# The last stage of a two-layer trunk (combine of two expert rows, final norm): rolled with two buffers, or written out with sixteen

## What is computed

```python
# end of hier_moe, layer 1: each token's two expert rows, weighted, are added to the residual x
x = x + hier_moe(h, ...)
# and then the final norm
inv = lax.rsqrt(jnp.mean(x * x, axis=-1, keepdims=True) + 1e-6)
y = x * inv * final_norm
```

## Time and profile before

| | us |
|---|---|
| median of 3 runs | 3452.34 |
| the 3 runs | 3441.14, 3452.34, 3454.4 |
| span of the profiled execution | 3440.8 |

### The profile page before, as it was taken

One profiled execution on the slowest core, in us unless ns is written; L12 is line 12 of the kernel. 1 busy time (PEld: TensorE's weight loads), 2 busy tenths in 40 slices (PEclk: granted clock), 3 DMA queues, 4 the chain that ended last, 5 costly groups with the idle time before them and its releaser, 6 DMA issues. The chain is left out here.

```text
span 3440.8 us, 53421 instructions
## 1 busy us (share of the span) xinstructions
PE 2953.7 (86%) x16322; PEld 2534.4 (74%) x16323; DVE 1949.2 (57%) x2787; ACT 1384.3 (40%) x2388; POOL 950.1 (28%) x894
## 2 busy tenths in 40 slices
PE   6999999999999999769999589999959589999700
PEld 5887788778877887658888489888849478889600
DVE  6548754876387638732211555576647777665433
ACT  5334333433343334321111145666624256666411
POOL 1013200320032003300000144465624256554332
PEclk8999999999999999979999689999979789999955
DMA  5323332323232323253222467798667569987555
GB/s 185 107 86 109 97 112 80 110 97 112 79 108 99 117 74 110 99 172 102 106 98 86 141 217 277 281 323 317 245 210 261 181 237 323 330 301 280 180 184 196
DMA packets 332189, 587.33 MB, mean 171 GB/s; under 512 B 23104, under 2 KB 206912, under 8 KB 332096
## 3 DMA queue, kind: packets, MB, share of 16 engines
q1 hardware_dynamic: 294944, 450.92, 38.3%
q0 software_dynamic: 37152, 135.28, 11.0%
HBM read 427.27 MB, written 158.86 MB: 170 GB/s over the span
## 5 line engine op out<-in xcount | busy, mean ns | idle before, releaser
L57 PE MATMUL ret_ps_p<-ret_w_hi,ret_x_hi 128*128 128x512 f32 x1536 | 606.7, 395 | 15.6 <-DVE ret_x_lo L1077 12.6
L59 PE MATMUL ret_ps_p<-ret_w_hi,ret_x_lo 128*128 128x512 f32 x1536 | 600.0, 391 | 0.0
L58 PE MATMUL ret_ps_p<-ret_w_lo,ret_x_hi 128*128 128x512 f32 x1536 | 599.2, 390 | 0.0
L1077 DVE TENSOR_TENSOR ret_x_lo<-hT,ret_x_hi 128x1024 fp32r<-128x1024 f32 x193 | 368.4, 1909 | 249.9 <-ACT ret_x_hi L1017 248.4
L57 PE MATMUL moe_ps_gu<-moe_gu_hi,moe_x_hi 128*128 128x256 f32 x1520 | 431.7, 284 | 3.5 <-DVE moe_x_lo L553 2.8
L58 PE MATMUL moe_ps_gu<-moe_gu_lo,moe_x_hi 128*128 128x256 f32 x1520 | 429.1, 282 | 0.0
L59 PE MATMUL moe_ps_gu<-moe_gu_hi,moe_x_lo 128*128 128x256 f32 x1520 | 429.1, 282 | 0.0
L985 POOL TENSOR_TENSOR ret_state_lo<-ret_state,ret_state_hi 128x1024 fp32r<-128x1024 f32 x68 | 176.6, 2597 | 838.2 <-ACT ret_state_hi L1007 838.2
L463 POOL TENSOR_TENSOR moe_dn_lo<-moe_raw_down,moe_dn_hi 128x1024 fp32r<-128x1024 f32 x128 | 366.5, 2881 | 17.7 <-ACT moe_dn_hi L498 16.9
L57 PEld LDWEIGHTS ret_ps_p<-ret_w_hi,ret_x_hi 128*128 128x128 f32 x1536 | 289.4, 188 | 77.2 <-DVE ret_x_lo L1077 14.4
L59 PEld LDWEIGHTS ret_ps_p<-ret_w_hi,ret_x_lo 128*128 128x128 f32 x1536 | 289.1, 188 | 61.7
(11 more groups left out here) (220 smaller groups left out, 5630.6 us busy)
## 6 DMA issues: line engine op xcount, KB each, us to landing
moe_raw_gate<-in_moe_w_gate SPq DMA_DIRECT2D x64, 1024.0 KB, 7.4
moe_raw_up<-in_moe_w_up SPq DMA_DIRECT2D x64, 1024.0 KB, 10.9
moe_raw_down<-in_moe_w_down SPq DMA_DIRECT2D x64, 1024.0 KB, 10.3
expert_rows<-moe_y POOLq DMA_DIRECT2D x95, 512.0 KB, 7.5
raw<-in_ret_w_in SPq DMA_DIRECT2D x20, 1024.0 KB, 9.0
qk_rows<-ret_qk_out SPq DMA_DIRECT2D x64, 256.0 KB, 2.1
ret_qk_out<-qk_rows SPq DMA_DIRECT2D x64, 256.0 KB, 3.0
gate_rows<-ret_gate SPq DMA_DIRECT2D x64, 256.0 KB, 2.0
```

Source lines behind the costliest of these rows:

```text
L57: pe.matmul(out, x_hi, w_hi, start=first, stop=False)
L58: pe.matmul(out, x_hi, w_lo, start=False, stop=False)
L59: return pe.matmul(out, x_lo, w_hi, start=False, stop=last)
L1077: dve.tensor_tensor(x_lo[par][:, :, :], hT[:, :, ds(t * P, P)], x_hi[par][:, :, :].bitcast(F32), ALU.subtract).then_inc(x_split, 1)
```

## The change

`final_phase` no longer uses `Combine`. It has buffers of its own for each of the 16 tiles: `x_res`, `picked0`, `picked1` (64 KB of each partition each), and 16 columns each of `sumsq`, `mean_eps` and `rstd`. All 16 tiles are written out on every engine. Gathers read their row numbers from `row_of_token` itself, so `index` and its copies are gone. Loads and gathers of tiles 0 to 3 are issued at the start, those of tile t+4 as soon as the second multiply-add of tile t is done. The multiply-adds and the norm write into `x_res`, the squares go to `picked0`, and the store reads `x_res`; no buffer is used twice.

```diff
-        comb = Combine(s, x_in_rows, y_rows, weight, row_of_token, gain)
+        x_res = s.slots("x_res", TILES, [P, D])
+        picked = [s.slots(f"picked{k}", TILES, [P, D]) for k in range(TOPK)]
...
         @blk.sync
         def _(sp):
-            comb.load_gain(sp)
-            comb.load(sp, 0, 0)
-
-            def step(i, par, has):
-                if has[0] and not (isinstance(i, int) and i >= TILES - 1):
-                    comb.load(sp, i + 1, 1 - par)
-                if has[1]:
-                    sp.wait_ge(y_ready, i)
-                    sp.dma_start(out[ds((i - 1) * P, P), :], y[1 - par][:, :]).then_inc(y_stored[1 - par], 16)
-            staggered(sp, step, 2)
...
+            load(0)
+            sp.dma_start(gain_b[:, :], gain.rearrange("(a d) -> a d", a=1).to_broadcast([P, D])
+                         ).then_inc(gain_landed, 16)
+            for t in range(1, LEAD):
+                load(t)
+            for t in range(TILES):
+                if t + LEAD < TILES:
+                    sp.wait_ge(x2_ready, t + 1)
+                    load(t + LEAD)
+                if t >= 1:
+                    sp.wait_ge(y_ready, t)
+                    sp.dma_start(out[(t - 1) * P:t * P, :], x_res[t - 1][:, :]).then_inc(y_stored, 16)
...
         @blk.gpsimd
         def _(pool):
             s.clear_before(pool)
+            def gather(t):
+                for k in range(TOPK):
+                    pool.indirect_dma_start(
+                        out=picked[k][t][:, :], out_offset=None, in_=y_rows[:, :],
+                        in_offset=bass.IndirectOffsetOnAxis(ap=row_of_token[:, k, t:t + 1], axis=0),
+                    ).then_inc(picked_landed[k][t % LEAD], 16)
+
+            for t in range(LEAD):
+                gather(t)
             pool.memset(power[:, :], -0.5).then_inc(power_set, 1)
             pool.wait_ge(power_set, 1)
-            comb.gather(pool, 0, 0)
-            comb.gather(pool, 1, 1)
...
+            for t in range(TILES):
+                if t + LEAD < TILES:
+                    pool.wait_ge(x2_ready, t + 1)
+                    gather(t + LEAD)
+                pool.wait_ge(sumsq_ready, t + 1)
+                pool.tensor_scalar(mean_eps[:, t:t + 1], sumsq[:, t:t + 1], 1.0 / D, EPS, ALU.mult, ALU.add
+                                   ).then_inc(mean_ready, 1)
+                pool.wait_ge(mean_ready, t + 1)
+                pool.tensor_tensor(rstd[:, t:t + 1], mean_eps[:, t:t + 1], power[:, :], ALU.pow
+                                   ).then_inc(rstd_ready, 1)
...
         @blk.vector
         def _(dve):
...
+                dve.wait_ge(picked_landed[k][t % LEAD], landed(t))
+                dve.scalar_tensor_tensor(out=x_res[t][:, :], in0=picked[k][t][:, :], scalar=weight[:, k, t:t + 1],
+                                         in1=x_res[t][:, :], op0=ALU.mult, op1=ALU.add
+                                         ).then_inc((half_ready, x2_ready)[k], 1)
...
+            dve.wait_ge(gain_landed, 16)
+            for t in range(TILES):
+                add(t, 0)
+                add(t, 1)
+                if t >= 1:
+                    norm(t - 1)
+            norm(TILES - 1)
```

More of the change, by code:

```diff
@@ L1759, in final_phase @@
 def final_phase(nc, past, x_in_rows, y_rows, weight, row_of_token, gain, out):
+    LEAD = 4
     with Scope(nc, "final", past) as s:
-        comb = Combine(s, x_in_rows, y_rows, weight, row_of_token, gain)
+        x_res = s.slots("x_res", TILES, [P, D])
+        picked = [s.slots(f"picked{k}", TILES, [P, D]) for k in range(TOPK)]
+        gain_b = s.sb("gain_b", [P, D])
+        sumsq = s.sb("sumsq", [P, TILES])
+        mean_eps = s.sb("mean_eps", [P, TILES])
+        rstd = s.sb("rstd", [P, TILES])
@@ L1763, in final_phase @@
         power = s.sb("power", [P, 1])
-        y = s.slots("y", 2, [P, D])
+        gain_landed = s.sem("gain_landed")
+        x_landed = [s.sem(f"x_landed{i}") for i in range(LEAD)]
+        picked_landed = [[s.sem(f"picked{k}_landed{i}") for i in range(LEAD)] for k in range(TOPK)]
         power_set = s.sem("power_set")
+        half_ready = s.sem("half_ready")
+        x2_ready = s.sem("x2_ready")
+        sumsq_ready = s.sem("sumsq_ready")
+        mean_ready = s.sem("mean_ready")
+        rstd_ready = s.sem("rstd_ready")
@@ L1766, in final_phase, with landed, load @@
         y_ready = s.sem("y_ready")
-        y_stored = [s.sem(f"y_stored{i}") for i in range(2)]
+        y_stored = s.sem("y_stored")
         blk = s.block()
+        def landed(t):
+            return 16 * (t // LEAD + 1)
         @blk.sync
         def _(sp):
-            comb.load_gain(sp)
-            comb.load(sp, 0, 0)
-            def step(i, par, has):
-                if has[0] and not (isinstance(i, int) and i >= TILES - 1):
-                    comb.load(sp, i + 1, 1 - par)
-                if has[1]:
-                    sp.wait_ge(y_ready, i)
-                    sp.dma_start(out[ds((i - 1) * P, P), :], y[1 - par][:, :]).then_inc(y_stored[1 - par], 16)
-            staggered(sp, step, 2)
-            for i in range(2):
-                sp.wait_ge(y_stored[i], 8 * TILES)
+            def load(t):
+                sp.dma_start(x_res[t][:, :], x_in_rows[t * P:(t + 1) * P, :]).then_inc(x_landed[t % LEAD], 16)
+            load(0)
[10 more added lines that the diff above has]
+                    sp.dma_start(out[(t - 1) * P:t * P, :], x_res[t - 1][:, :]).then_inc(y_stored, 16)
+            sp.wait_ge(y_ready, TILES)
+            sp.dma_start(out[(TILES - 1) * P:TILES * P, :], x_res[TILES - 1][:, :]).then_inc(y_stored, 16)
+            sp.wait_ge(y_stored, 16 * TILES)
@@ L1800, in _ @@
         @blk.scalar
         def _(act):
[L1802 to L1805, removed]
+            for t in range(TILES):
+                act.wait_ge(x2_ready, t + 1)
+                act.activation(picked[0][t][:, :], x_res[t][:, :], ACT.Square, accum_out=sumsq[:, t:t + 1]
+                               ).then_inc(sumsq_ready, 1)
         @blk.vector
         def _(dve):
-            dve.wait_ge(comb.gain_landed, 16)
@@ L1811, in norm, with add @@
[L1811 to L1822, removed]
+            def add(t, k):
+                if k == 0:
+                    dve.wait_ge(x_landed[t % LEAD], landed(t))
+                else:
+                    dve.wait_ge(half_ready, t + 1)
+                dve.wait_ge(picked_landed[k][t % LEAD], landed(t))
+                dve.scalar_tensor_tensor(out=x_res[t][:, :], in0=picked[k][t][:, :], scalar=weight[:, k, t:t + 1],
+                                         in1=x_res[t][:, :], op0=ALU.mult, op1=ALU.add
+                                         ).then_inc((half_ready, x2_ready)[k], 1)
@@ new lines, in norm @@
+            def norm(t):
+                dve.wait_ge(rstd_ready, t + 1)
+                dve.scalar_tensor_tensor(out=x_res[t][:, :], in0=x_res[t][:, :], scalar=rstd[:, t:t + 1],
+                                         in1=gain_b[:, :], op0=ALU.mult, op1=ALU.mult).then_inc(y_ready, 1)
+            dve.wait_ge(gain_landed, 16)
+            for t in range(TILES):
+                add(t, 0)
[3 more added lines that the diff above has]
+            norm(TILES - 1)
```

## The result

| | before | after |
|---|---|---|
| median us | 3446.74 (4 runs, 3440.54 to 3454.4) | 3356.24 (4 runs, 3353.66 to 3357.71) |
| span of the profiled execution | 3440.8 | 3355.1 |
| final phase, from SP's first issue in it to the end | 3263.47 to 3440.8: 177.3 | 3265.85 to 3355.1: 89.2 |

The ratio is 0.9733, 95% interval 0.9707 to 0.9759. The sign and the place were right, and the size was not. The final phase alone accounts for the gain: it is 88.1 us shorter, while the phases before it ended 2.4 us later in this execution.

The account below looks back on a forecast made before the run. The final phase was taken as a chain of latencies that becomes DMA-bound: 101.7 us to the last landing plus 9.7 makes 111.4 instead of 176.5, 65 less. So 3452.3 - 65 = 3387 us, range 3366 to 3414.

Parts of the forecast that it names:

- What bounds the kernel: Final phase, 176.5 us: nothing is full, a chain of latencies with only one pair of gathers under way, period 10.5 us.
- The price of the traffic: Final phase as DMA-bound: 34.08 MB in 105 us (325 GB/s), the middle of 101.4 by rate and 108.9 by packet time.
- The place on the path: Final phase: 101.7 us of traffic up to the last landing, then an unchanged 9.7 us; 111.4 in all, 65 less.
- DVE, ACT and POOL as the next limit: Per tile of the final phase: DVE 4.1 us, POOL 3.8, ACT 1.06, all covered by 6.6 us of traffic.
- signs of being wrong altogether: In the profile after: the phases before moved, or DVE or POOL had no waits left.
- Indexing, buffers, in place: Final phase: indexing from the resident table keeps the 1.17 us issue; DVE takes the same duration in place or not.
- The loop through the lead: Gather of tile t+4 waits for tile t's second multiply-add: 11.2 us of latency, covered by 26 us of queued work.
- The slowest engine: Rival, chance 0.20: bursts keep their length because the same one or two DMA engines trail; phase 132.4 us, kernel 3408.
- The fast queue: Rival, chance 0.11: longer packets were only a lone burst's price; traffic at 374 GB/s, phase 98.0 us, kernel 3374.
- No running ahead: Rival, chance 0.05: POOL's queue holds one pair at a time; only copies and gaps go, 16 us less, kernel 3436.
- The slower case: Rival, chance 0.04: eight scattered gathers hinder each other, q0 packets lengthen; costs from factor 1.95, at 2.3 kernel 3475.
- the cap on the rate: Skill's 358 GB/s per core, traffic an estimated 95 us; taken as no cap, since the trace reached 374 GB/s.

Follow-up runs that it names:

- a lead of one: Changed kernel with gathers and loads issued one tile ahead instead of four: final phase 169.9 us, median 3434.44 us, ratio 0.996.
- half of the stores: Changed kernel without the stores of the even tiles, 29.9 MB of traffic instead of 34.1: final phase 86.0 us, median 3352.0 us, ratio 0.972.
- rings of eight: Changed kernel with eight reused buffers instead of sixteen for x_res and both gathers: final phase 89.5 us, median 3355.99 us, ratio 0.973.
- lead 2: Changed kernel with gathers and loads issued two tiles ahead instead of four: final phase 108.9 us, median 3372.67 us, ratio 0.978.

## Why the prediction was wrong in size

**What bounds the kernel.** Right. The old kernel was a chain of latencies with one pair under way; putting back that wait alone costs 52 us, and a lead of one 81.

**The price of the traffic.** This is the step that failed: 105 us (325 GB/s) for the traffic, against 34.08 MB at 417 GB/s, 82 us. It had two sources, and both were wrong in the same direction.

The rate of 336 GB/s came from a dense stretch of the expert phase. That stretch carries other packets and has a hole. The view of its DMAs in the kernel before (40 slices of 1.25 us, then packet counts):

```profile
GB/s 408 415 416 324 390 118 0 0 108 308 253 306 354 363 274 265 406 423 406 384 382 361 348 350 383 416 426 416 359 355 353 347 355 406 421 416 406 336 348 347
DMA packets 9978, 16.82 MB, mean 336 GB/s; under 512 B 338, under 2 KB 7717, under 8 KB 9978
```

Three quarters of its packets are under 2 KB, those of this phase 4 KB; two slices are at 0, others over 400. It was not full all the time, and its fullest slices (421 to 426) had this phase's rate. Whether the slices near 350 are slower for their shorter packets no run shows. The row that had the answer was in the prediction: 438 GB/s in one microsecond of this phase's own traffic. I used it as an argument about engines, not as a price.

The packet time kept today's packet lengths ("if each keeps its length"). They did not stay: q0's shortened as its queue stopped running dry. (The 17.50 MB of q0 in the earlier trace rows hold 0.7 MB of the phase before; within the phase q0 moves 16.78.) The sum of all packets fell from 0.58 x 177.3 = 103 us to 0.95 x 89.25 = 85 us of the 16 engines. Had I known 85, dividing by the 0.94 would have given 90, and by the 1.03 that was reached 82.

Up to the last landing I had 101.7 us. Measured, it is 3265.85 + about 0.8 to 3347.3, 80.6 us: 21 of the 23 us by which the phase came out shorter than the 111.4 forecast. The median lies 31 us under the 3387; the other 8 are no matter of the phase. The sum put the median 11.5 us above the profiled span, and after the change it is 1.1 above, while the phases before ended 2.4 later (11.5 - 1.1 - 2.4 = 8.0).

**The place on the path.** Nearly right. The tail, from the last landing on, was priced at 9.7 and is 7.8:

```profile
3347.36 1.28 DVE L1849 SCALAR_TENSOR_TENSOR final_x_res<-final_picked,weight,final_x_res 128x1024 f32<-128x1024 f32 x1 [0.86 <-DMA final_picked<-expert_rows,row_of_token]
...
3350.77 1.28 DVE L1855 SCALAR_TENSOR_TENSOR final_x_res<-final_x_res,final_rstd,final_gain_b 128x1024 f32<-128x1024 f32 x1 [0.93 <-POOL final_rstd L1831]
3352.09 0.33 SPq L1805 DMA_DIRECT2D out_y<-final_x_res  x1
```

The first multiply-add of the last tile no longer waits for its second gather, so only one of the two lies behind the landing: 1.3 of the 1.9 us.

**DVE, ACT and POOL as the next limit.** This term was mis-sized too. POOL was priced at 3.8 us per tile and needs 4.5, since a gather started behind a norm just begun takes 2.02 us; and "nothing" for the later root became 10.7 us of waits on DVE. With 6.6 us of traffic per tile this would have been nothing; with the real 5.0 it sets the pace up to 3327 and nearly the end, as half of the stores showed. Of the signs of being wrong altogether one came near: POOL had hardly a wait left in the middle. DVE's waits for gathers were to be 2 to 3 us per tile and were 3.7 in all after the first. My floor of 66 us by DVE was not to be had: DVE and POOL hold each other up at 4.5.

**Indexing, buffers, in place.** The forecast gave them nothing of their own, and they bring nothing: index copies back 88.4, rings of eight 89.5, the norm in place 1.28 us as before. Only buffers too few, six, cost something (18 us), which the sum did not ask. That the written-out code is worth something by itself (13.7 us in the old order) I had not priced at all; what it is worth in the new order was not tried.

**The loop through the lead.** Right as far as it went: 11.2 us forecast for it, 9.7 measured as the period at lead 1; at lead 2 it does not give the whole loss, as said above. It was also right that four tiles are more than needed.

**The rivals.** The slowest engine (3408) falls: the phase took 89.2 us and not the 132.4 of the bursts end to end, with the DMA share at 1.03 in its middle. The fast queue (3374, given 0.11) had the mechanism that the runs show, that long packets were the price of bursts with nothing queued behind them; its rate was still too low, since 374 GB/s came from the expert phases too. No running ahead (3436) falls: POOL issued eight gathers in 10.7 us at the start (3269.61 to 3280.35), as forecast, and a gather landed 12.2 us after its issue in the median, not the 15 or more. The slower case falls: q0's packets became shorter by a factor 144 / 205 = 0.70, not longer by 1.95. As to the cap on the rate, the Trainium skill ("DMA: Bandwidth & Descriptors", Bandwidth) also has 425 GB/s, measured with the pair's other core idle; the 417 here agrees with that figure, and not with the 358 that I weighed.

## What to carry to other kernels

Price a stretch that will be bound by its traffic at the rate of the fullest microseconds of the same packets, and look at packet sizes and empty slices before a rate is borrowed from another phase. A queue that ran dry paid twice here, in the idle time and in long packets: three tiles in flight were enough here, and in the old buffers, where the next transfer is issued in an engine's order (26 us) mattered as much as the wait and the copies that were taken away (25 us). Before buying buffers, see which wait needs them: eight did the work of sixteen, and six did not. When one limit is lifted, price the next one as it will run, with the engines beside each other: here POOL's 3.8 us became 4.5, and taking away an eighth of the traffic gained only 3 us.

## What the runs showed of the hardware that I had not expected

- 4 KB rows, half of them gathered from scattered places, moved at 416 GB/s over 60 us (3280 to 3340, 25 MB), with q0 at 144 ns per packet against 205 in bursts; a gathered 4 KB packet took 161 ns and one of q1's plain copies 163.
- A gather issue on POOL took 0.94 us, and about the rest of the DVE instruction more when one with two SBUF operands was already running: 2.02 with 1.13 us left of it. One that began after the gather did not lengthen it.
- The same instructions written out instead of rolled shortened a phase bound by landings by 13.7 us of 177.
